# Recurrence of a hybrid decoder: level products and diagonal in column groups of 32 keys, gathered in a narrow buffer

## What is computed

```python
G = jnp.cumsum(gc, axis=1)
diff = G[:, :, None] - G[:, None, :]
decay = jnp.exp(jnp.where(causal, diff, NEG_INF))
A = jnp.einsum('bthd,bshd,btshd->bhts', qc, kc, decay)
o = jnp.einsum('bhts,bshv->bthv', A, vc) + jnp.einsum('bthd,bhdv->bthv', qc * jnp.exp(G), S)
S_new = jnp.exp(G_last)[..., None] * S + jnp.einsum('bshd,bshv->bhdv', kc * jnp.exp(G_last[:, None] - G), vc)
```

## Time and profile before

| What | Value |
| --- | --- |
| median of 3 runs | 3034.33 us (3031.73 to 3035.17) |
| the profiled execution | 3030.23 us, span 3028.5 us |
| busy in the span | PE 93%, PEld 78%, DVE 52%, ACT 33%, POOL 35% |
| mean granted TensorE clock | 0.956 of full speed |
| level products (line 1344), all | 1840 passes, 249.8 us |
| diagonal products (line 1351), all | 272 passes, 41.4 us |
| masked copies of the levels (line 1184) | 230, 121.5 us |

### The profile page before, as it was taken

How to read it: one execution, slowest core, us unless ns; L and a number is a source line. 1 busy time by engine, 2 the same in 40 slices (tenths; PEclk the granted TensorE clock), 3 DMA queues, 4 the chain that set the end, 5 groups by cost and what they waited for, 6 DMA issues and landing times. The chain is left out here.

```text
span 3028.5 us, 42852 instructions
## 1 busy us (share of the span) xinstructions
PE 2803.7 (93%) x15186; PEld 2351.7 (78%) x15186; DVE 1589.3 (52%) x3037; ACT 1009.5 (33%) x2154; POOL 1058.1 (35%) x940
## 2 busy tenths in 40 slices
PE   6999868999999699999959999589999997899998
PEld 5777647888888578888757877478888886788887
DVE  4566654676667552222236666646676665622222
ACT  3333332444444331111123333424444443311111
POOL 1212112555555443333212221125555544433332
PEclk9999978999999799999979999789999997999999
DMA  4111221000000422222141111310000004121121
GB/s 156 42 42 36 102 69 53 28 21 24 21 28 14 175 68 76 79 88 88 59 163 51 32 41 66 110 53 22 28 21 24 21 21 155 67 68 68 68 68 45
DMA packets 94463, 186.18 MB, mean 61 GB/s; under 512 B 10640, under 2 KB 55952, under 8 KB 92304
## 3 DMA queue, kind: packets, MB, share of 16 engines
q1 hardware_dynamic: 94384, 185.14, 18.4%
HBM read 135.10 MB, written 51.90 MB: 62 GB/s over the span
## 5 line engine op out<-in xcount | busy, mean ns | idle before, releaser
L103 PE MATMUL r_Z<-w_rec_high,w_rec_xh 128*128 128x512 f32 x1088 | 446.3, 410 | 38.7 <-POOL w_rec_xl L942 30.3
L103 PE MATMUL r_Z<-w_rec_high,w_rec_xl 128*128 128x512 f32 x1088 | 430.7, 396 | 0.0
L103 PE MATMUL r_Z<-w_rec_low,w_rec_xh 128*128 128x512 f32 x1088 | 429.8, 395 | 0.0
L103 PE MATMUL a_Z<-w_attn_high,w_attn_xh 128*128 128x512 f32 (+1 forms) x816 | 303.1, 371 | 0.0
L103 PE MATMUL a_Z<-w_attn_low,w_attn_xh 128*128 128x512 f32 (+1 forms) x816 | 291.7, 358 | 0.0
L103 PE MATMUL a_Z<-w_attn_high,w_attn_xl 128*128 128x512 f32 (+1 forms) x816 | 290.9, 357 | 0.0
L951 POOL TENSOR_TENSOR r_qE<-r_qT,r_E 128x256 f32<-128x256 f32 x230 | 188.7, 820 | 282.2 <-ACT r_E L1037 157.1
L1344 PEld LDWEIGHTS r_LV<-r_qE,r_kE 128*128 128x128 f32 x1840 | 249.1, 207 | 48.6 <-POOL r_kE L951 27.3
L1344 PE MATMUL r_LV<-r_qE,r_kE 128*128 128x64 f32 x1840 | 249.8, 290 | 32.3 <-POOL r_kE L951 22.7
L103 PEld LDWEIGHTS r_Z<-w_rec_high,w_rec_xh 128*128 128x128 f32 x1088 | 209.2, 192 | 78.7 <-issue 40.2
L1184 DVE COPY_PREDICATED r_A<-levels,r_LV 128x256 f32<-128x256 int32 x230 | 121.5, 528 | 245.6 <-issue 161.9
(11 more groups left out here) (253 smaller groups left out, 5645.9 us busy)
## 6 DMA issues: line engine op xcount, KB each, us to landing
w_attn_xraw<-dram_xT SPq DMA_DIRECT2D x34, 512.0 KB, 3.6
r_xraw<-dram_xT SPq DMA_DIRECT2D x34, 512.0 KB, 3.4
o_mraw<-dram_mixT SPq DMA_DIRECT2D x34, 512.0 KB, 4.4
dram_y_all<-o_hb SPq DMA_DIRECT2D x34, 512.0 KB, 2.9
w_rec_whole<-dram_w_in SPq DMA_DIRECT2D x16, 1024.0 KB, 12.3
w_attn_whole<-dram_w_in SPq DMA_DIRECT2D x16, 640.0 KB, 7.9
dram_mixT<-a_mixT SPq DMA_DIRECT2D x136, 64.0 KB, 2.1
dram_mixT<-r_u SPq DMA_DIRECT2D x34, 256.0 KB, 2.0
```

The costliest lines, as they stand in the source:

```text
L103: mm = pe.matmul(out, a[:, c, :], b[:, c, :], start=(first and c == chunks[0] and a is xh and b is wh), stop=(last and c == chunks[-1] and ...
```

## The change

Level products and the diagonal are made for 32 keys at a time, as matmuls with 32 weight columns that write to the four groups of 32 partitions in turn.

- Levels 64 and 32 (`h >= NEAR`): only the blocks of 32 keys that lie in a first half get a matmul, over h queries: 8 matmuls of 32x64 and 8 of 32x32 instead of 4 and 4. Their results are copied straight into A with plain copies (one of 64 partitions, two of 32).
- Levels 16 to 1: 16 matmuls of 32x16 instead of 4 of 128x64. They are taken with masks of a new form into a narrow buffer `near`, 128 keys x 4 heads x 32 queries, 64 elements a partition instead of 256.
- Diagonal: 16 matmuls of 32x32 instead of 4 of 128x128; the masked copy goes into `near` (128 elements instead of 512) and raises the new semaphore `near_done`.
- New, `take_near`: VectorE waits for `near_done` and copies `near` into A with four copies of 32 partitions; the last raises `A_done`.
- TensorE's transpose of `kh` waits for `near_done` instead of `A_done`; the outputs wait for `A_done`.
- The tables are loaded as eight small blocks, 12 loads instead of 6 before the first weights.

```diff
@@ VectorE, take_level
+                    src = LV[l % 2]
+                    if h >= NEAR:
+                        dve.wait_ge(S["level_mm"], passed(n) + l + 1)
+                        for r in range(0, P, 2 * h):
+                            op = dve.tensor_copy(A[r:r + h, :, r + h:r + 2 * h],
+                                                 src[r:r + h, 0:GH * h].rearrange("p (g t) -> p g t", g=GH))
+                    else:
+                        mask = C["near"][:, NEAR_LEVELS.index(h), :].rearrange("p (n t) -> p n t", t=h)\
+                            .unsqueeze(1).to_broadcast([P, GH, NEAR // (2 * h), h])
...
+                        op = dve.copy_predicated(near[:, :, :].rearrange("p g (n s t) -> p g n s t", s=2, t=h)[:, :, :, 1, :], mask,
+                                                 src[:, 0:GH * NEAR // 2].rearrange("p (g n t) -> p g n t", g=GH, t=h))
+                    op.then_inc(S["level_took"], 1)
+
+                def take_near(n, levels):
+
+                    dve.wait_ge(S["level_took"], passed(n) + len(levels))
+                    wait_apart(dve, S["dve_passed"], S["diag_ps"], n + 1)
+                    dve.copy_predicated(near[:, :, :], C["diagonal"][:, :].unsqueeze(1).to_broadcast([P, GH, NEAR]),
+                                        M[:, 0:GH * NEAR].rearrange("p (g t) -> p g t", g=GH)).then_inc(S["near_done"], 1)
+                    dve.wait_ge(S["near_done"], n + 1)
+                    for r in range(0, P, NEAR):
+                        op = dve.tensor_copy(A[r:r + NEAR, :, r:r + NEAR], near[r:r + NEAR, :, :])
+                    op.then_inc(S["A_done"], 1)
@@ TensorE, level
                     for g in range(GH):
-                        mm = pe.matmul(LV[i][:, 64 * g:64 * g + 64], kE[i][:, g * P:(g + 1) * P],
-                                       qE[i][:, g, :], start=True, stop=True)
+                        if h >= NEAR:
+                            for r in range(0, P, NEAR):
+                                block, q = r // (2 * h), slice(r // (2 * h) * h, r // (2 * h) * h + h)
+                                if r % (2 * h) < h:
+                                    mm = pe.matmul(LV[i][r:r + NEAR, g * h:g * h + h],
+                                                   kE[i][:, g * P + r:g * P + r + NEAR], qE[i][:, g, q], start=True, stop=True)
+                        else:
+                            for r in range(0, P, NEAR):
+                                mm = pe.matmul(LV[i][r:r + NEAR, g * 16:g * 16 + 16], kE[i][:, g * P + r:g * P + r + NEAR],
+                                               qE[i][:, g, r // 2:r // 2 + 16], start=True, stop=True)
@@ TensorE, diagonal
                     for g in range(GH):
-                        mm = pe.matmul(M[:, g * P:(g + 1) * P], kT[:, g, :], qT[:, g, :], start=True, stop=True)
+                        for r in range(0, P, NEAR):
+                            mm = pe.matmul(M[r:r + NEAR, g * NEAR:(g + 1) * NEAR], kT[:, g, r:r + NEAR], qT[:, g, r:r + NEAR],
+                                           start=True, stop=True)
@@ TensorE, transpose_kh and output_and_update
-                    pe.wait_ge(S["A_done"], n + 1)
+                    pe.wait_ge(S["near_done"], n + 1)
...
+                    pe.wait_ge(S["A_done"], n + 1)
@@ constants
+                for r in range(0, P, NEAR):
+                    rows = slice(r, r + NEAR)
+                    sp.dma_start(C["near"][rows, :, :], dram["levels"][rows, -len(NEAR_LEVELS):, r // 2:(r + NEAR) // 2])\
+                        .then_inc(S["const_in"], 16)
+                    sp.dma_start(C["diagonal"][rows, :], dram["diagonal"][rows, rows]).then_inc(S["const_in"], 16)
```

More of the change, by code:

```diff
@@ L52 @@
 LEVELS = (64, 32, 16, 8, 4, 2, 1)
+NEAR = 32
+NEAR_LEVELS = (16, 8, 4, 2, 1)
 DEC_LEVELS = (4, 2, 1)
@@ L66 @@
     x_split yT_ps yT_sb yT_st y_done y_st0 y_st1 z_f z_g z_kv z_q z_v zeroed zqf_sb
-    folded divided unfolded attnT_done summed ssq_ps gT_ps v_moved
+    near_done folded divided unfolded attnT_done summed ssq_ps gT_ps v_moved
 """
@@ L846, in recurrence_phase @@
         qG, kh, khT = sb("qG", [P, GH, P]), sb("kh", [P, GH, P]), sb("khT", [P, GW])
+        near = sb("near", [P, GH, NEAR])
         A, state, u = sb("A", [P, GH, P]), sb("state", [P, GH, DK]), sb("u", [P, GW])
@@ L1175, in take_level @@
                 def take_level(n, l, h):
[L1176 to L1182, removed]
@@ L1183, in take_level @@
-                    wait_apart(dve, S["dve_passed"], S["level_mm"], passed(n) + l + 1)
-                    dve.copy_predicated(to, mask, src).then_inc(S["level_took"], 1)
+                    src = LV[l % 2]
[7 more added lines that the diff above has]
+                            .unsqueeze(1).to_broadcast([P, GH, NEAR // (2 * h), h])
+                        if l:
+                            dve.wait_ge(S["level_took"], passed(n) + l)
+                        wait_apart(dve, S["dve_passed"], S["level_mm"], passed(n) + l + 1)
+                        op = dve.copy_predicated(near[:, :, :].rearrange("p g (n s t) -> p g n s t", s=2, t=h)[:, :, :, 1, :], mask,
+                                                 src[:, 0:GH * NEAR // 2].rearrange("p (g n t) -> p g n t", g=GH, t=h))
@@ L1214, in middle @@
                         take_level(n, l, levels[l])
[L1215 to L1218, removed]
+                    take_near(n, levels)
                 def new_state(n):
@@ L1255, in _ @@
                 dve.memset(A[:, :, :], 0.0)
+                dve.memset(near[:, :, :], 0.0)
                 dve.memset(kE[0][:, :], 0.0)
@@ L1433, in _ @@
                 pe.wait_ge(S["v_copied"], 1)
+                pe.wait_ge(S["A_done"], 1)
                 for g in range(GH):
@@ L1869, in _ @@
             def _(sp):
-                for to, table in ((C["ident"], dram["ident"]), (C["diagonal"], dram["diagonal"]),
-                                  (C["batch_rows"], dram["batch_rows"])):
+                for to, table in ((C["ident"], dram["ident"]), (C["batch_rows"], dram["batch_rows"])):
                     sp.dma_start(to[:, :], table[:, :]).then_inc(S["const_in"], 16)
-                for to, table in ((C["levels"], dram["levels"]), (C["sinks"], dram["sinks"]), (logits, dram["logits"])):
+                for to, table in ((C["sinks"], dram["sinks"]), (logits, dram["logits"])):
                     sp.dma_start(to[:, :, :], table[:, :, :]).then_inc(S["const_in"], 16)
+                for r in range(0, P, NEAR):
[3 more added lines that the diff above has]
+                    sp.dma_start(C["diagonal"][rows, :], dram["diagonal"][rows, rows]).then_inc(S["const_in"], 16)
                 following.load(sp, dram, 0, 0, following.chunks)
-                sp.wait_ge(S["const_in"], 6 * 16)
+                sp.wait_ge(S["const_in"], 12 * 16)
             @block.vector
@@ L1887, in op @@
                     dve.wait_ge(S["const_dve"], done)
-                dve.wait_ge(S["const_in"], 6 * 16)
+                dve.wait_ge(S["const_in"], 12 * 16)
                 op(dve.tensor_copy(C["identb"][:, :], C["ident"][:, :]))
@@ L1935, in program @@
         C = dict(
-            ident=sb("ident", [P, P]), identb=sb("identb", [P, P], BF16), diagonal=sb("diagonal", [P, P], I32),
-            levels=sb("levels", [P, len(LEVELS), P // 2], I32), batch_rows=sb("batch_rows", [P, DEC_BATCH]),
+            ident=sb("ident", [P, P]), identb=sb("identb", [P, P], BF16), diagonal=sb("diagonal", [P, NEAR], I32),
+            near=sb("near", [P, len(NEAR_LEVELS), NEAR // 2], I32), batch_rows=sb("batch_rows", [P, DEC_BATCH]),
             sinks=sb("sinks", [P, DEPTH, HEADS + 4]), neg_half=sb("neg_half", [P, GH]),
```

## The result

The changed kernel takes 3073.02 us (median; 3069.35 to 3086.61) beside 3034.75 for the kernel before on the same chip, a ratio of 1.0138 (95%: 1.0121 to 1.0155). The forecast was 3000. The profiled execution took 3071.02 us, span 3069.2, against a span of 3028.5 before.

What follows compares the result with a forecast made beforehand. TensorE's queue was taken to bound the kernel, with VectorE's chain limiting the gain. 28 steps x (0.5 + 0.42 + 0.18) = 30.8 us, plus 6, less 2.9, gave 34 us saved: 3000 us, range 2968 to 3034.

Steps and rivals of the forecast that it cites:

- the price of the four copies: VectorE's copies from near to A before lsig: 0.28 us each, 1.12 together, with lsig taken 0.15 us later.
- The rival: Copies to A wait for GpSimd's subtraction: lsig 2.3 us late, step 1.05 us longer, 3063 us; chance 0.09.
- The clock falls: TensorE's idle lowers its clock: one projection at 1.2 GHz in each step would cost over 100 us; chance 0.02.
- S2: Step segment from the transpose of u to levels 2 and 3 of the next tile, 5.91 us; no saving forecast.
- S3: Step segment from levels 2 and 3 to the transposes of q and f, 1.72 us; 0.42 us saved.
- S4: Step segment from the transposes of q and f to level 4, 3.66 us; no saving forecast.
- S5: Step segment from level 4 to the next levels 5 and 6, 3.66 us; 0.18 us saved.
- the 0.1 of entry: Cost on TensorE of entering a block of small matmuls: 0.09 us, counted as 0.1, possibly 0.
- S1: Step segment from levels 5, 6 and the diagonal to the transpose of u, 18.61 us; 0.5 us saved.
- A pass has a floor price: TensorE's small passes cost 25 ns each, so gains vanish and the diagonal is late: 3055 us; chance 0.05.
- Ends and start: Outside steady steps: 6 us gained (0 to 9) at first and last tiles, 2.9 us lost to 12 initial loads.
- the 2955 case: TensorE stays the only bound because VectorE's chain has unseen slack: 79 us gained, 2955 us; chance 0.07.

Runs made afterwards that it cites:

- the filler run: Changed kernel plus ten unused 512-column matmuls on TensorE ahead of level 0 in each steady step; 3036.32 us, ratio 1.0017 to the kernel before.
- the run with the copy from PSUM: Kernel before plus one VectorE copy of 32x128 from PSUM into an unread tile behind the diagonal's masked copy; 3033.78 us, ratio 1.0001.

## Why the prediction was wrong, step by step

**The step that failed** is the price of the four copies: "four copies of 32 partitions, no row for this form, taken at 0.28 each, 1.12 together". Where nothing holds them they take 0.22 as copies and 0.28 as reductions, four of these in 1.15 without overlap, so that size was good; the second one waited for GpSimd and took 2.35, and `lsig` came 1.87 us later than before instead of 0.15. The upper bound went wrong in the same way: 0.75 for each, from the masked copies, which read PSUM. The rows of before have no copy from SBUF to SBUF beside GpSimd, and I took the nearest form on the same engine without asking whether its source decides. The rival had the mechanism, "The copies near to A fall beside GpSimd's subtraction (933.65 to 936.06) and wait for its end", with a chance of 0.09 on the ground "they are slowed there, not stopped". They are stopped. The port rule of the Trainium skill, quoted above, speaks of exactly this pair and should have set that chance far higher; it is also the rule against this change that I should have weighed.

**How far the rival was right.** It put `lsig` 2.3 us late; it is 1.87. It put its step 1.05 longer. With the clock restored the step is 34.06, 0.49 longer, 0.56 less than that: `lsig` is 0.43 less late, and the rest lies in the hand-over to the transposes of u (0.08 in after, 942.29 less 941.18 + 1.03, for 0.15) and in smaller terms. Alone it would have given about 3036 (the filler run), not 3063. The remaining 37 us are nearly all that the change lost against the kernel before, and they are the rival "The clock falls", taken at 0.02 "because TensorE now idles about 1 us in each step". The premise was too small: with the chain late it idles 3.15 us, in two pieces. I had treated these two as separate cases, while one brings the other.

**The times add up.** Counted from level 5 to level 5, the 28 steps of the profiled execution cost 54.5 us more than before, 1.95 each: 0.49 from the chain (13.8 us, which the filler's 28 steps cost too), and 1.46 (40.7 us) that leave with the filler, so the clock's. The rest gave 13.8 back: 54.5 - 13.8 = 40.7, the difference of the spans.

**The other terms**, read from the kernel with the copies on ScalarE, where the failed step is out of the way. Its gain is 57 us, not 34:
- S2 and S3 together save 7.63 - 7.26 = 0.37 us, for 0.42 in the forecast; the transposes of q and f do wait for ScalarE's copy, in after too (0.45, at 950.79). S4 and S5 save 0.21, for 0.18. Both terms held, though the 0.1 of entry is paid ahead of each block, in S2 and S4.
- S1 saves 1.12 for 0.5, and this is the mis-sized term. From `lsig` to the end of u it is 734.10 + 1.03 - 721.04 = 14.09 us, for 14.49 before: the copy of khT is out of the way and gives 0.40, forecast 0.36. `lsig` is 0.33 earlier instead of 0.15 later, as its hand-over from ScalarE takes 0.03 and nothing of VectorE's is in the way. And the transposes follow u by 0.06 instead of 0.45, where I had kept 0.15.
- A pass costs less than taken. Levels 5 and 6 take 957.90 to 958.49 for 64 passes, 9 ns each, for 13 to 18 in the forecast from the earlier trace rows, which have 64 columns a pass. It did not matter: the diagonal was never late for VectorE. The rival "A pass has a floor price" is out, and the rows decide against the 25 ns that the prediction drew from the Trainium skill.
- Ends and start: SP issues the first weights at 6.37 us, as forecast (6.4), and in after TensorE's first matmul starts 2.66 us later (24.60 for 21.94). Outside the 28 steps the profiled executions of after and of its five variants gain 4.7 to 13.8 us net of that, for 3.1 in the forecast and 6 at its cheap end. This remainder is known to a few us only: the same part of the span is 2.1 us longer than before in the run with the copy from PSUM, though that changes next to nothing there. What gives the gain was not taken apart.

**The range** ended at 3034 and left the slower side out, 0.16 by my count. With the copies' price between 0.28 and the length of the instruction they wait for, both ends possible, it should have reached 3063; and 3073 lies outside that as well, as long as the clock is not taken in as a consequence of the late chain. Two figures of the working don't come out, and nothing hangs on them: half way from 2988 to the 2955 case is 2972, not 2968, and at 25 ns a pass the diagonal would be 1.1 us later than in the sum, not 0.8.

## What to carry to other kernels

Before adding or moving a VectorE copy whose source and target are both in SBUF, look at what GpSimd runs at that moment: the copy can take as long as GpSimd's instruction lasts. Written as a reduction over an axis of one, given to ScalarE, or with GpSimd's long instruction ordered behind it, the same move brought this kernel from 3073 to between 2976 and 2979 us. And where TensorE alone was busy without a gap, a chain behind it that becomes late can cost more than its lateness: ask what the new wait does to the granted clock.

## What the runs showed that was not expected

- A 32x128 fp32 copy from SBUF to SBUF takes 0.22 us and took up to 2.357 beside GpSimd's 2.40 us subtraction; as a reduction 0.283 at most, from PSUM 0.267 at most, in the same place.
- Waits of 2.30 and 0.85 us in a step of 35 to 36 brought TensorE's granted clock down to 0.93 over the stretch; a wait of 0.84 to 0.91 alone left it at 1.00. In layer 2 of after some steps took 34.0 us, as long as with the filler, with the same queues: with these waits the clock falls in most steps, not in all, and what decides this I don't know.
- Passes of 16 columns in four column groups start 9 ns apart (64 in 0.59 us), and a block of 96 of them with the drain takes 0.98 us.
